# Layer 1's gate and attention output kept feature-major in a two-layer fp32 trunk

## The reference

```
# layer 0 (pooling mixer)
h = rms_norm(x, norm0);  u, z = split(h @ w_in0, 2)
y = pool_mixer(u, w_pool0, pool_scale0) * silu(z);  x = x + y @ w_out0
# layer 1 (attention; one block of 256 keys, so plain causal attention)
h = rms_norm(x, norm1);  q, k, v, z = split(h @ w_in1, 4)
q = rope(rms_norm(heads(q), q_norm1));  k = rope(rms_norm(heads(k), k_norm1))
o = softmax(causal(q @ k.T * 128**-0.5)) @ v
out = x + (o * silu(z)) @ w_out1
```

## Time and profile before

| | us |
|---|---|
| median of 3 runs (lowest, highest) | 431.68 (431.66, 431.73) |
| profiled execution, its own time | 431.68 |
| its span | 429.9 |
| busy PE / DVE / ACT / GpSimd | 423.5 / 281.4 / 231.0 / 163.1 |

### The profile page before, as it was taken

How to read it: one execution, slowest core, us unless ns; L and a number is a source line. 1 busy time by engine, 2 the same in 40 slices (tenths; PEclk the granted TensorE clock), 3 DMA queues, 4 the chain that set the end, 5 groups by cost and what they waited for, 6 DMA issues and landing times.

```text
span 429.9 us, 5672 instructions
## 1 busy us (share of the span) xinstructions
PE 423.5 (99%) x2214; PEld 362.7 (84%) x2214; DVE 281.4 (65%) x340; ACT 231.0 (54%) x406; POOL 163.1 (38%) x111
## 2 busy tenths in 40 slices
PE   8999999999999999999999999999999999999997
PEld 8979898988888888888788888888888888888885
DVE  3866898688985544356664798447983579836532
ACT  5745545444554443578447765477654786546310
POOL 0077417267000000089804595055940559300000
PEclk9999999999999999999999999999999999999999
DMA  8987578645455747436833667236672355731002
GB/s 273 386 285 272 195 244 314 214 159 178 167 197 175 217 137 221 123 94 204 295 101 99 186 184 226 91 100 193 196 216 84 99 191 196 246 105 41 2 0 98
DMA packets 38026, 75.25 MB, mean 175 GB/s; under 512 B 1648, under 2 KB 1776, under 8 KB 38000
## 3 DMA queue, kind: packets, MB, share of 16 engines
q1 hardware_dynamic: 37280, 73.83, 52.8%
q10 hardware_dynamic: 720, 1.07, 0.8%
HBM read 73.84 MB, written 1.05 MB: 174 GB/s over the span
## 4 chain that ended last, share of the span: by engine, by line
PE 85%; POOL 7%; DMA 2%; DVE 2%; ACT 1%; SPq 1%; issue 1%; DVEq 0%
PE acc L599 23%; PE acc L601 22%; PE acc L600 22%; PE aux L654 4%; POOL wide L344 3%; PE acc L644 3%; PE acc L643 3%; PE acc L641 3%; DMA raw<-in_w_in_dram 2%; PE aux L738 2%; POOL k_s L337 1%; PE aux L745 1%; SPq L232 1%; PE aux L757 1%; PE aux L756 1%; PE aux L755 1%
## 5 line engine op out<-in xcount | busy, mean ns | idle before, releaser
L836 DVE TENSOR_TENSOR w_lo<-raw,w_hi 128x2048 fp32r<-128x2048 f32 x65 | 165.2, 2548 | 57.6 <-ACT w_hi L367 57.5
L367 ACT ACTIVATE w_hi<-raw 128x2048 fp32r<-128x2048 f32 x64 | 121.9, 1915 | 28.3 <-PE acc L601 21.7
L599 PE MATMUL acc<-w_hi,hT_hi 128*128 128x512 f32 x320 | 127.7, 399 | 1.0 <-DVE w_lo L836 1.0
L601 PE MATMUL acc<-w_hi,hT_lo 128*128 128x512 f32 x320 | 124.9, 390 | 0.0
L600 PE MATMUL acc<-w_lo,hT_hi 128*128 128x512 f32 x320 | 124.6, 389 | 0.0
L601 PEld LDWEIGHTS acc<-w_hi,hT_lo 128*128 128x128 f32 x320 | 60.1, 188 | 13.0
L599 PEld LDWEIGHTS acc<-w_hi,hT_hi 128*128 128x128 f32 x320 | 60.2, 188 | 12.9 <-DVE w_lo L836 1.4
L600 PEld LDWEIGHTS acc<-w_lo,hT_hi 128*128 128x128 f32 x320 | 60.2, 188 | 11.5
L599 PE MATMUL acc<-w_hi,aT_hi 128*128 128x512 f32 x160 | 63.7, 398 | 0.0
L601 PE MATMUL acc<-w_hi,aT_lo 128*128 128x512 f32 x160 | 62.4, 390 | 0.0
L600 PE MATMUL acc<-w_lo,aT_hi 128*128 128x512 f32 x160 | 62.3, 389 | 0.0
(11 more groups left out here) (125 smaller groups left out, 593.7 us busy)
## 6 DMA issues: line engine op xcount, KB each, us to landing
raw<-in_w_in_dram SPq DMA_DIRECT2D x46, 1024.0 KB, 5.5
raw<-in_w_out_dram SPq DMA_DIRECT2D x16, 1024.0 KB, 5.0
raw<-in_w_pool_dram SPq DMA_DIRECT2D x4, 1024.0 KB, 5.5
raw<-in_w_in_dram SPq DMA_DIRECT2D x8, 256.0 KB, 7.4
wide<-in_xT_dram ACTq DMA_DIRECT2D x4, 256.0 KB, 6.6
xs<-in_x_dram SPq DMA_DIRECT2D x1, 1024.0 KB, 7.7
out_dram<-ysb SPq DMA_DIRECT2D x4, 256.0 KB, 2.0
wide<-in_table_dram SPq DMA_DIRECT2D x1, 256.0 KB, 8.9
```

Of the source, the lines that this page charges most:

```text
L367: act.activation(w_hi[:, slot, :], raw[:, slot, :], ACT.Copy).then_inc(hi_made, 1)
L599: pe.matmul(a, shi, whi, start=first and k == 0, stop=False)
L601: ins = pe.matmul(a, slo, whi, start=False, stop=last and k == GK - 1)
L836: dve.tensor_tensor(w_lo[:, slot, :], raw[:, slot, :], w_hi[:, slot, :].bitcast(F32), ALU.subtract).then_inc(w_split, 1)
```

## The change

Layer 1's z is computed feature-major (features on partitions, tokens along the row), weights stationary. Its weights are laid out on the host as eight pieces of all 1024 rows by 256 columns, `w_gate`; a group has two, one for each pair of heads. `gate_pair` runs, per 128 features and per 128 rows, a 256-column matmul of `w_lo` with `hT_hi` and a 512-column one of `w_hi` with `hT_hi` and `hT_lo` side by side (which is why `hT` is one tile now). The two halves of the PSUM bank are added afterwards: ACT copies the second (`z_lo_part`), DVE adds (`z_sum`) and multiplies by half the rstd, which is spread over all partitions once (`spread_rstd(1)`, two diagonal passes on DVE). Tanh and the gate's product follow per pair. In the order of ACT and DVE the second pair's steps come at the head of the next group.

In the attention v is the stationary operand, so the output comes feature-major, as `aT` wants it; y1's transposes are gone, and the split is made per head from `y1T` in SBUF. The division by the row sum is done on the probabilities before they are turned (`probs_norm`). The squares of q and k are cut in halves with the head's work between them. Five products per group alternate between the two accumulator pairs (`side`), and the PSUM tiles are parts of two tiles of four banks (`quad`).

```diff
-                pe.wait_ge(exp_made, HPG * g + h + 1)
+                pe.wait_ge(probs_made, HPG * g + h + 1)
...
-                pe.matmul(aux[3][:, 0:P], probsT[:, 0:P], v[0], start=True, stop=True)
-                pe.matmul(aux[3][:, P:2 * P], probsT[:, P:2 * P], v[0], start=True, stop=False)
-                pe.matmul(aux[3][:, P:2 * P], probsT[:, 2 * P:3 * P], v[1], start=False,
-                          stop=True).then_inc(o_ready, 1)
+                o = aux[3][:, 0:SEQ]
+                pe.matmul(o[:, P:SEQ], v[1], probsT[:, SEQ:3 * P], start=True, stop=False, skip_group_check=True)
+                pe.matmul(o, v[0], probsT[:, 0:SEQ], start=False, stop=True, skip_group_check=True).then_inc(o_ready, 1)
...
+            def tile_of_two(out_, n, c, h, start, stop):
+                pe.matmul(out_[:, 0:SEQ], w_lo[:, n % RING, c:c + P], h[:, 0, :], start=start, stop=False,
+                          skip_group_check=True)
+                return pe.matmul(out_, w_hi[:, n % RING, c:c + P], h.rearrange("p a s -> p (a s)"), start=False,
+                                 stop=stop, skip_group_check=True)
...
+            def gate_pair(g, p):
+                n = N_L1 + 8 * g + 6 + p
+                pe.wait_ge(w_split, n + 1)
+                pe.wait_ge(qkv_out[1 + p], TT * (g + 1))
+                for f in range(2):
+                    for k in range(KD):
+                        ins = tile_of_two(acc[side(g, 3 + p)][f], n, k * 2 * P + f * P, hT[:, k], k == 0, k == KD - 1)
+                ins.then_inc(w_used, 1)
 
             def layer1(g, first):
-                for j in range(8):
+                for j in range(6):
                     which = j // 2
-                    free = {0: (x1_made, TT) if first else (qkv_out[2], TT * g),
-                            1: (x1_made, 2 * TT) if first else (gate_made, TT * (GROUPS + g)),
-                            2: (qkv_out[0], TT * (g + 1)), 3: (qkv_out[1], TT * (g + 1))}[which]
+                    free = {0: (x1_made, TT) if first else (z1_made, 2 * g - 1),
+                            1: (x1_made, 2 * TT) if first else (z1_made, 2 * g),
+                            2: (qkv_out[0], TT * (g + 1))}[which]
...
-                    if j == 6:
-                        turn_qk(g, 0, first)
-                    if j == 7:
-                        if not first:
-                            turn_y1(g - 1, g)
-                        turn_qk(g, 1, first)
+                    if first and j == 3:
+                        spread_rstd(1)
+                gate_pair(g, 0)
+                turn_qk(g, 0, first)
+                gate_pair(g, 1)
+                turn_qk(g, 1, first)
...
+            def probs_norm(g, h):
                 dve.wait_ge(exp_made, HPG * g + h + 1)
                 chain.done(dve.reciprocal(row_inv[:, h, :], row_sum[:, h, :]))
+                dve.tensor_scalar(probs[:, 0:P], probs[:, 0:P], row_inv[:, h, 0:1], 1.0, ALU.mult, ALU.mult)
+                dve.tensor_scalar(probs[:, P:3 * P], probs[:, P:3 * P], row_inv[:, h, 1:2], 1.0, ALU.mult,
+                                  ALU.mult).then_inc(probs_made, 1)
...
+            def y1_rest(g, h):
+                dve.wait_ge(y_hi, 8 + HPG * g + h + 1)
+                dve.tensor_tensor(aT_lo[:, HPG * g + h, :], y1T[:, h, :], aT_hi[:, HPG * g + h, :].bitcast(F32),
+                                  ALU.subtract).then_inc(y_split, 1)
...
+            def z_sum(g, p):
+                dve.wait_ge(z1_lo_copied, 2 * g + p + 1)
+                if g > 0:
+                    dve.wait_ge(y1_made, HPG * (g - 1) + 2 * p + 2)
+                if (g, p) == (0, 0):
+                    dve.wait_ge(rstd_b_made, 2)
+                z = gate1T[:, p]
+                chain.done(dve.tensor_tensor(z, quad[side(g, 3 + p)][:, 0:2, 0:SEQ], z_lo, ALU.add))
+                dve.tensor_tensor(z, z, rstd_b[:, :].unsqueeze(1).to_broadcast([P, 2, SEQ]),
+                                  ALU.mult).then_inc(z1_made, 1)
```

More of the change, by code:

```diff
@@ L556, in _ @@
             act.wait_ge(rstd_made, 2)
-            layer1(0, attend=False)
-            for g in range(1, GROUPS):
-                layer1(g, attend=True)
+            for g in range(GROUPS):
+                layer1(g)
             last = GROUPS - 1
[L563 to L570, removed]
+            z_lo_part(last, 1)
+            static_hi(N_OUT1 + 3)
+            tanh_z(last, 1)
+            exp_scores(last, 0)
+            static_hi(N_OUT1 + 4)
+            exp_scores(last, 1)
+            probs_out(last, 0)
+            static_hi(N_OUT1 + 5)
+            exp_scores(last, 2)
+            probs_out(last, 1)
+            static_hi(N_OUT1 + 6)
+            y1_hi(last, 0)
+            exp_scores(last, 3)
+            probs_out(last, 2)
+            static_hi(N_OUT1 + 7)
+            y1_hi(last, 1)
+            probs_out(last, 3)
+            y1_hi(last, 2)
+            y1_hi(last, 3)
         @block.tensor
@@ L678, in h_needed, with spread_rstd @@
                 return need
[L680 to L681 removed]
+            def spread_rstd(layer=0):
+                pe.wait_ge(diag_made, layer + 1)
                 for t in range(TT):
[L683 removed]
+                    ins = pe.matmul(aux[2 - 2 * layer][:, t * P:(t + 1) * P], square_ones[:, :], diag[:, t, :], start=True, stop=True)
                 ins.then_inc(rstd_spread, 1)
@@ new lines, in layer1 @@
+                w(1)
+                if g == 0:
+                    dve.wait_ge(rstd_made, 2)
+                    for t in range(TT):
+                        ins = dve.tensor_scalar(diag[:, t, :], ident[:, :], rstd[:, t:t + 1], 1.0, ALU.mult, ALU.mult)
+                    ins.then_inc(diag_made, 1)
+                if g > 0:
+                    head_max(b, 2)
+                    y1_out(b, 0)
+                    probs_norm(b, 2)
+                w(2)
+                if g > 0:
+                    y1_rest(b, 0)
+                    head_max(b, 3)
+                    y1_out(b, 1)
+                    probs_norm(b, 3)
@@ L1075, in _ @@
-            y1_lo_bank(last, 1)
+            z_sum(last, 1)
+            weight_lo(N_OUT1 + 3, 3)
+            gate_out(last, 1)
+            head_max(last, 0)
+            probs_norm(last, 0)
+            weight_lo(N_OUT1 + 4, 0)
+            head_max(last, 1)
+            probs_norm(last, 1)
+            weight_lo(N_OUT1 + 5, 1)
+            head_max(last, 2)
+            y1_out(last, 0)
+            probs_norm(last, 2)
+            weight_lo(N_OUT1 + 6, 2)
+            y1_rest(last, 0)
+            head_max(last, 3)
@@ L1076, in _ @@
+            y1_out(last, 1)
+            probs_norm(last, 3)
+            weight_lo(N_OUT1 + 7, 3)
+            y1_rest(last, 1)
+            y1_out(last, 2)
+            y1_rest(last, 2)
+            y1_out(last, 3)
+            y1_rest(last, 3)
             for half in range(2):
                 for t in range(TT):
-                    product_ready(dve, t, 30 + half, N_OUT1 + 6 + half)
-                    dve.wait_ge(y_turned, 16)
+                    product_ready(dve, t, 26 + half, N_OUT1 + 6 + half)
```

254 lines of the change are left out of this document (119 added, 135 removed).

## The result

The changed kernel takes 435.44 us against 431.71 for the one before: ratio 1.0087, 95% interval 1.0070 to 1.0105. It is 0.9% slower, clear of noise. The forecast was 435.4. The span of its profiled execution is 433.6, 3.7 more than 429.9.

The account below looks back on a forecast made before the run. TensorE was taken to bound the kernel, with k's path 3.6 us from the seams. Three periods +3.6, group 0 +0.9 and the last stage -0.75 gave +3.75 on 431.68: 435.4 us, range 430.4 to 439.4.

Parts of the forecast that it names:

- the k path at the seams: K's path through ACT, GpSimd and DVE to PE's turns: a later rotary sum makes each of three periods 1.2 us longer.
- group 0: Layer 1's first group, without attention beside it: z's sum +0.6 and two diagonal passes 0.3, together +0.9 us (0.5 to 1.2).
- the last stage: From the last seam to the end: fewer transposes, less a wait for head 0's probabilities, -0.75 us (-1.2 to 0).
- PE's saving: PE work per group: transposes 0.84 and values product 0.08 saved, gate's narrow matmuls 0.21 added, so 0.71 us shorter.
- The walk through ACT and DVE: Hand-offs between ACT and DVE in group 2, priced in order: GpSimd starts k 3.4 us later (2.8 to 4.5).
- the spare time: Before PE's turns of k in the kernel before: k's path could come 3.6 us later without PE waiting.
- The step that failed: GpSimd's k chain stretched 0.8 us by y1's rest passes on DVE, so the rotary sum ends 4.2 later, at s+52.8.
- What the seam costs: Behind k's rotary sum on DVE, z's sum takes two passes and a wait, 1.45 us, before the next q product.
- Rival 1: K's path fits: GpSimd starts k less than 2.28 us late and no seam stalls, 429.0 us; chance 0.18.
- Rival 3: Exclusion of DVE and GpSimd at full price: delay 4.1, stretch 1.26, period +2.4, 439.6 us; chance 0.14.
- rival 2: Break-even: delay 3.0 and no stretching of GpSimd, a stall of 0.7 eats the 0.71 saved, 431.8 us; chance 0.14.
- Rival 4: In the gate a 256-wide matmul costs a 512-wide slot: +3.4 us per group on PE, 441.4 us; chance 0.04.

Follow-up runs that it names:

- x2: The changed kernel with all eight of k's squares on ACT ahead of head 3's exponentials, not four before and four behind: 428.95 us, ratio 0.9938.
- x8: The kernel before the change with only k's squares split around head 3's exponentials and head 2's turned probabilities, all ahead of w(3): 431.82 us, ratio 1.0006.
- x3: The changed kernel with the low part of y1 made for only 2 of 256 columns, the rest left out: 433.85 us, ratio 1.0047.
- x4: The changed kernel with DVE taking head 2's maximum before w(1)'s low part instead of behind it, except in group 0: 433.21 us, ratio 1.0033.
- x10: The changed kernel with GpSimd's multiplication of k by its rstd made for only 2 of 128 columns of each head: 430.00 us, ratio 0.9958.
- x1: The changed kernel with DVE preparing w(6)'s low part behind k's rotary sum and z's sum instead of ahead of them: 432.89 us, ratio 1.0028.
- x6: x2 and x1 in one, so k's squares whole and w(6)'s low part behind z's sum: 428.32 us, ratio 0.9920.

## Why the prediction was right

**The direction and the size** came from the right place, the k path at the seams: per period +1.36 for +1.2 forecast, group 0 +0.49 for +0.9, the last stage -0.88 for -0.75. The total hits partly because these errors cancel: +0.45, -0.41 and -0.13.

**PE's saving** was put at 0.71 per group. x2, in which PE waits nowhere between the seams, has 52.18 for 53.04: 0.86. The gate's step of one 256-wide and one 512-wide matmul is 0.35, as said. The missing 0.15 is in the starts of PE in group 2 of the two kernels: y1's turns were 0.88 for the 0.84 taken, everything up to the first gate pair is 0.25 shorter where 0.08 was put down for the values product, and the gate with q's turns is 0.27 longer for 0.21.

**The walk through ACT and DVE** held up to GpSimd's start. Head 2's maximum ended at s'+23.1, my upper bound and not the 22.5 that I took; from there to GpSimd's start it was 9.9, as walked. The delay against the kernel before was thus 4.1, within 2.8 to 4.5. In the kernel before that maximum ended at s+21.9; no run tells how much of the 1.3 between them is `probs_norm`, which none takes off DVE's queue. x8 shows that a delay alone, 1.4 in the kernel before, costs nothing within the spare time. x2 shows that without the split the delay fits, too.

**The step that failed** is who comes last. I let GpSimd's chain grow from 18.4 to 19.2 and release the rotary sum at s+51.6, and named a chain of over 19 us as a sign of being right. It took 16.7 and was done at s'+49.8. The rotary sum started at s'+51.8 all the same, since DVE's own queue came last: 1.26, 0.95 and 1.52 for three rests, 3.39 for the last w_lo. In the window of k's chain I had booked the exclusion on GpSimd alone. That 51.8 and 51.6 agree is luck: GpSimd's start 0.6 later than I took, its chain 2.5 shorter, and DVE 2.1 behind its end. The Trainium skill's "SBUF — State Buffer", section "Summary: rules for kernel authors", says that where DVE has two SBUF inputs and GpSimd reads SBUF, the second to issue blocks fully until the first finishes. x3 agrees, with the two-column pass that ends with GpSimd's step, and with 2.28 and 3.42 there for 3.39 and 1.48 in the change. The sum would have needed both queues.

**What the seam costs** from there on was right. The two passes and the wait behind the rotary sum were put at 1.23 + 1.45 = 2.68; q starts 2.60 behind the start of the rotary sum. It is so in group 2 of all four kernels whose PE waits there for z's sum:

| kernel | rotary sum starts, in the group | + 2.60 | period |
|---|---|---|---|
| change | 51.84 | 54.44 | 54.44 |
| x3 | 51.21 | 53.81 | 53.82 |
| x4 | 51.04 | 53.64 | 53.64 |
| x10 | 50.15 | 52.75 | 52.74 |
| x2, no wait | 49.56 | 52.16 | 52.18 |

In x2 the rotary sum would allow 52.16, and PE's own work takes 52.18.

**The wait for y1's PSUM tile** (L799, 0.84 per group by the starts) I did not name. It is part of the same queue: `y1_out` of head 2 stands behind w_lo 3.14 and a rest 1.26. In the change it adds nothing to the period, by the table above: the seam comes at the same distance from the rotary sum in x4 and x10, which lack it. Without it PE would have waited that much longer at the seam. Where the seam is freed, in x1, it does cost.

**Group 0**: z's sum stands where it was said and costs 0.49 for 0.6, and that goes in x1, x6 and x7. The two diagonal passes did not stretch GpSimd: its chain ends at 213.91, and at 213.90 before.

**The rivals.** Rival 1 (429.0, all fits) is what x2 is: the change with four squares moved. It was never far away: the order as written gave a delay of 4.1, 2.28 was allowed, and x2's is 1.5. Rival 3 had the delay (4.1), but its stretched GpSimd chain did not come, nor did rival 2's delay of 3.0. Rival 4 is excluded by the 0.35 step. The range's upper end, 439.4, is not the sum of its high terms: 3 x 2.8 + 1.2 + 0 on 431.68 is 441.3, and rival 3's 439.6 lay outside, too. What stays open is how much of x2's gain is GpSimd's earlier start and how much DVE's; no run moved the start of one alone.

## What to carry to other kernels

When work is taken off the bounding engine, ask what spare time its feeders had and what the same edit spends of it: here 0.86 per group was won on PE, while the rotary sum started 4.5 us later in the group, where 3.6 had been spare. Walk a path through in-order engines with every hand-off, and book a shared resource on both engines. A wait inside a long burst of work on a feeder is worth looking for: here moving four squares ahead of it won 6.5 us.

## What was not expected of the hardware

A DVE pass with two SBUF inputs pays beside GpSimd by waiting, and a short one as much as a longer one: in x3 two columns took 0.15 us alone and 0.70 to 1.25 beside it, in the change 256 columns 0.42 alone and 0.95 to 1.52 beside it. A scaling of 128 columns by a scalar per partition (a pointer scalar), with one SBUF input, took 1.32 us beside GpSimd against 0.29 alone in the changed kernel:

```profile
295.47 1.32 DVE L1030 TENSOR_SCALAR probs<-probs,row_inv 128x128 f32<-128x128 f32 x1
...
302.36 0.29 DVE L1030 TENSOR_SCALAR probs<-probs,row_inv 128x128 f32<-128x128 f32 x1
```

The prediction had such an instruction free of GpSimd. The section of the Trainium skill that it names, "Who interferes with whom" in "SBUF — State Buffer", exempts one SBUF input only outside DVE's 2-port performance modes. Whether this scaling ran in such a mode no run shows; 128 more columns took it 0.06 us (0.35 for 256), and 256 more columns took two-input passes 0.27 (0.42 and 0.69).
